# A 2-layer transformer with an RWKV block: the end of a finished channel tile put behind the next tile's first inversion matrices, bias rows copied in one piece, bias loads issued behind evacuations

## The reference, cut to what matters

```python
for l in range(2):                                   # first kind
    mod = silu(c) @ ada_w[l] + ada_b[l]              # 6 x 1024 numbers: shift, scale, gate, twice
    h = rms_norm(x) * (1 + sc_m) + sh_m
    proj = h @ w_in[l]                               # q, k, v of three attentions, three gates
    o_na  = neighborhood_attention(...)              # 4 heads; bias rpb (4,15,31) by row and column offset
    o_mla, o_gqa = latent and grouped attention
    x = x + g_m * ((sig(ga)*(o_na@wa) + sig(gb)*(o_mla@wb) + sig(gc)*(o_gqa@wc)) @ w_out)
    x = x + g_f * ffn(rms_norm(x) * (1 + sc_f) + sh_f)
x = rms_norm(x)
p = rms_norm_2(x) @ w_in_2                           # second kind
y_a = b_a * conv3(c_a * x_a);  y_b = rg_lru(conv4(x_b)) * gelu(g_b)
# RWKV-7: state = state*w_t + (state@-kk)(kk*a) + v k ; y = state@r, chunks of 128 tokens
yc = group_norm(y)*lnx_g + lnx_b + bonus;  y_c = yc * g_c
x = x + (gate_a*y_a + gate_b*y_b + gate_c*y_c) @ w_out_2
x = x + relu(rms_norm_2(x) @ w1)**2 @ w2;  out = rms_norm_2(x)
```

## Time and profile before

| | |
|---|---|
| median of 3 runs | 3166.22 us (3163.53 to 3168.85) |
| profiled execution | 3169.7 us; its span, first to last instruction, 3167.9 us |
| PE busy | 2930.3 us, 92% |
| DVE busy | 1698.2 us, 54% |
| ACT busy | 698.0 us, 22% |
| POOL busy | 1279.5 us, 40% |
| mean granted TensorE clock | 0.973 |

### The profile page before, as it was taken

One profiled execution on the slowest core, in us unless ns is written; L12 is line 12 of the kernel. 1 busy time (PEld: TensorE's weight loads), 2 busy tenths in 40 slices (PEclk: granted clock), 3 DMA queues, 4 the chain that ended last, 5 costly groups with the idle time before them and its releaser, 6 DMA issues.

```text
span 3167.9 us, 44134 instructions
## 1 busy us (share of the span) xinstructions
PE 2930.3 (92%) x18104; PEld 2265.4 (72%) x18104; DVE 1698.2 (54%) x2263; ACT 698.0 (22%) x1183; POOL 1279.5 (40%) x940
## 2 busy tenths in 40 slices
PE   2899988999998999999999969999999999999997
PEld 1666666787786767777888757777777777778786
DVE  4488775566513776445443274665465466463352
ACT  2343220200002443201000033223233323220000
POOL 1323334455564333354555522333233323345553
PEclk8899999999999999999999989999999999999999
DMA  8644556577766233364555532333233333445553
GB/s 271 180 136 141 190 200 200 178 239 236 235 218 176 93 93 122 120 199 162 193 192 197 198 109 99 106 119 121 89 125 114 112 104 117 142 159 190 182 192 113
DMA packets 174631, 503.85 MB, mean 159 GB/s; under 512 B 41206, under 2 KB 56566, under 8 KB 174198
## 3 DMA queue, kind: packets, MB, share of 16 engines
q1 hardware_dynamic: 82800, 274.75, 26.7%
q0 software_dynamic: 67392, 218.40, 19.5%
q10 hardware_dynamic: 24262, 8.21, 1.6%
HBM read 280.76 MB, written 6.06 MB: 91 GB/s over the span
## 4 chain that ended last, share of the span: by engine, by line
PE 78%; DVE 10%; DMA 4%; issue 3%; POOL 2%; ACT 2%; ACTq 1%; SPq 0%; DVEq 0%; POOLq 0%
PE ps L327 22%; PE ps L328 20%; PE ps L329 20%; DMA raw<-in_weights_dram 4%; PE ps L1184 3%; PE ps L1015 2%; POOL wR L531 2%; PE ps L1025 2%; PE ps L1035 2%; PE ps L1229 1%; DVE work L1465 1%; DVE dB L1889 1%; DVE kB L1901 1%; PE ps L1328 1%; DVE yB L1862 1%
## 5 line engine op out<-in xcount | busy, mean ns | idle before, releaser
L327 PE MATMUL ps<-hR,wR 128*128 128x512 f32 x2320 | 960.6, 414 | 117.2 <-DVE hR L1472 52.1
L531 POOL TENSOR_TENSOR wR<-raw,wR 128x1024 fp32r<-128x1024 f32 (+3 forms) x468 | 1016.2, 2171 | 69.9 <-DMA wR<-raw 52.4
L522 POOL DMA_DIRECT2D wR<-raw x468 | 267.4, 571 | 1783.8 <-issue 1321.8
L328 PE MATMUL ps<-hR,wR 128*128 128x512 f32 x2320 | 916.7, 395 | 0.0
L329 PE MATMUL ps<-hR,wR 128*128 128x512 f32 x2320 | 916.1, 395 | 0.0
L327 PEld LDWEIGHTS ps<-hR,wR 128*128 128x128 f32 x2320 | 443.5, 191 | 249.5 <-issue 134.0
L329 PEld LDWEIGHTS ps<-hR,wR 128*128 128x128 f32 x2320 | 442.6, 191 | 97.2
L328 PEld LDWEIGHTS ps<-hR,wR 128*128 128x128 f32 x2320 | 444.6, 192 | 86.6 <-issue 4.8
L1428 DVE CUSTOM_DVE_ANT_0 raw<-raw,cs 128x1024 f32<-128x1024 f32 x96 | 165.0, 1728 | 72.1 <-DMA raw<-in_weights_dram 65.7
L557 ACT ACTIVATE sq<-xT 128x512 f32<-128x512 f32 x56 | 35.4, 633 | 493.8 <-DVE xT L1479 341.9
L1479 DVE SCALAR_TENSOR_TENSOR xT<-ps,lm,xT 128x512 f32<-128x512 f32 x32 | 24.0, 751 | 223.1 <-PE ps L329 223.1
(11 more groups left out here) (358 smaller groups left out, 4153.7 us busy)
## 6 DMA issues: line engine op xcount, KB each, us to landing
raw<-in_weights_dram SPq DMA_DIRECT2D x490, 512.0 KB, 3.3
wR<-raw POOLq DMA_DIRECT2D x394, 512.0 KB, 2.9
raw<-in_weights_dram SPq DMA_DIRECT2D x50, 128.0 KB, 2.9
wR<-raw POOLq DMA_DIRECT2D x50, 128.0 KB, 2.0
raw<-in_weights_dram SPq DMA_DIRECT2D x16, 256.0 KB, 3.2
wR<-raw POOLq DMA_DIRECT2D x16, 256.0 KB, 2.6
bias_toeplitz<-bias_rows ACTq DMA_DIRECT2D x8, 476.2 KB, 15.8
bias<-bias_toeplitz ACTq DMA_DIRECT2D x16, 224.0 KB, 5.7
```

The costliest lines, as they stand in the source:

```text
L327: mm(out, w_hi, r_hi, start=first, stop=False)
L328: mm(out, w_hi, r_lo, start=False, stop=False)
L522: pool.dma_start(wR[:, u, 0, 0:cols], raw[:, r % RING, 0:cols]).then_inc(hi_ready[u], 16)
L531: nc.gpsimd.tensor_tensor(wR[:, u, 1, 0:cols], raw[:, r % RING, 0:cols], wR[:, u, 0, 0:cols], ALU.subtract).then_inc(tile_ready, 1)
```

## The change

1. **Order of the stream.** Weight tile 0 stands before mod tile 14, weight tile 1 behind mod tile 15. The two rope tables (512 KB each) are no longer among the nine inputs that SP issues behind the first four tiles but are issued just before weight tile 3, with a semaphore of their own for which DVE waits before it uses the bias.
2. **Bias rows.** The four `toeplitz` DMAs of a layer become one: 64 copies of the layer's 60 rows, each a piece of 7620 numbers. The sliding by one number a partition is now in the reading pattern of the loads into `bias` (same shape, 64x14x64).
3. **Bias loads** are issued by ACT behind the evacuation of product 1 (four) and of product 2 (four), in both layers; layer 1's copy behind the evacuation of product 4.
4. **First two products of layer 0**: product 1 follows product 0 four steps behind. Layer 1 keeps the old order.
5. **RWKV**: `finish` is cut in two. `finish_y` (norm, bonus, times g) stays; the four instructions after it (gate, sum, two for `mR`) go behind the identity add. ACT takes g after `g_used`, and waits for `m_done` before it takes ca. The product for the bonus (`bnB`) goes from before the first X mask to behind the first T add. PE takes 22 steps before the LT matrices and 6 behind the L matrices, not 21 and 7.

```diff
-RAW.insert(N_FIRST - 1, ("tile", 1))
-RAW.insert(N_FIRST - 3, ("tile", 0))
+RAW.insert(N_FIRST - 2, ("tile", 0))
 for g_ in range(G_USED):
-    if g_ > 1:
+    if g_:
         RAW.append(("tile", g_))
...
+                if r == RAW_AT["tile", 3]:
+                    for dst, src in ((tab, tables1["axial"]), (tabm, tables1["rope"])):
+                        sp.dma_start(dst[:], src).then_inc(s_tab, 16)
...
-            def toeplitz(l):
-                for lh in range(4 * l, 4 * l + 4):
-                    act.dma_start(bass.AP(dram_toeplitz, GRID * 15 * SKEW * lh, [[SKEW, 15], [15 * SKEW + 1, GRID], [1, 127]]),
-                                  bass.AP(dram_bias, 127 * 15 * lh, [[127, 15], [0, GRID], [1, 127]])).then_inc(s_rows, 16)
+            def copy_rows(l):
+                act.dma_start(bass.AP(dram_copies, GRID * BIAS_ROWS * l, [[BIAS_ROWS, GRID], [1, BIAS_ROWS]]),
+                              bass.AP(dram_bias, BIAS_ROWS * l, [[0, GRID], [1, BIAS_ROWS]])).then_inc(s_rows, 16)
+            def load_bias(l, heads):
+                act.wait_ge(s_rows, 32 + 16 * (l + 1))
+                for h in heads:
+                    for half in range(2):
+                        first = GRID * BIAS_ROWS * l + (h * 15 + 1 - half) * 127 + GRID - 1
+                        act.dma_start(bias[64 * half:64 * half + 64, h],
+                                      bass.AP(dram_copies, first, [[BIAS_ROWS - 1, GRID], [127, 14], [1, GRID]])).then_inc(s_bias, 16)
...
                     if p in (2, 3):
                         turn(p - 2)
+                    if p in (1, 2):
+                        load_bias(l, (2 * p - 2, 2 * p - 1))
+                    if p == 4 and l == 0:
+                        copy_rows(1)
...
-                act.wait_ge(m_done, m + 1)
+                act.wait_ge(g_used, m) if m else None
                 take("g", m, gB[:])
...
+                act.wait_ge(m_done, m + 1)
                 take("ca", m, msum[:])
...
-            def pair_of_products(ts, p, H):
+            def pair_of_products(ts, p, H, lead=0):
+                slots, banks = {}, {}
+                for k in range(KD + lead):
+                    for j, kj in enumerate((k, k - lead)):
+                        if not 0 <= kj < KD:
+                            continue
+                        if kj == 0:
+                            slots[j], banks[j] = need_tile(Count(ts[j])), claim(Count(p + j))
+                        if j == 0:
+                            pe.wait_ge(h_ready, H + k + 1)
...
-                pair_of_products((TI, TI + 1), PR, H)
+                pair_of_products((TI, TI + 1), PR, H, 0 if l else 4)
...
-                fill(21)
+                fill(22)
                 pe.wait_ge(prep_ready, m + 1)
                 lt_blocks().then_inc(mat_ready, 1)
                 pe.wait_ge(y_sb, m) if m else None
                 l_blocks().then_inc(mat_ready, 1)
-                fill(7)
+                fill(6)
...
                 shift_in("k", m, 0, kB[:], W_MUK)
                 if m:
-                    finish(m - 1)
-                else:
-                    floor_k(0)
+                    finish_y(m - 1)
+                floor_k(m)
                 shift_in("v", m, 1, vB[:], W_MUV)
...
                 v.sync()
+                if m:
+                    finish(m - 1)
                 dve.wait_ge(shifted, 5 * m + 3)
-                STT(bnB[:], rB[:], vec(vec2, W_RK), kB[:], ALU.mult, ALU.mult).then_inc(bn_in, 1)
```

More of the change, by code:

```diff
@@ L19 @@
 GRID = 64
-SKEW = 127 + GRID - 1
+BIAS_ROWS = 4 * 15 * 127
 FFN = 2816
@@ L593, in _ @@
                 round_h(2 * KD * l, SH_M)
-                act.wait_ge(s_rows, 32 + 64 * (l + 1))
-                for half in range(2):
-                    for h in range(4):
-                        src = dram_toeplitz.ap()[l * 4 + h, :, 1 - half:15 - half, GRID - 1:127]
-                        act.dma_start(bias[64 * half:64 * half + 64, h], src).then_inc(s_bias, 16)
-                if l == 0:
-                    toeplitz(1)
                 def ended(p):
@@ L873, in h_lo @@
                 return hR[:, 1, k, :]
-            def pair_of_products(ts, p, H):
-                slots, banks = [need_tile(Count(t)) for t in ts], [claim(Count(p + j)) for j in range(2)]
-                for k in range(KD):
-                    pe.wait_ge(h_ready, H + k + 1)
-                    for j in range(2):
-                        mm = three_passes(MM, ps[:, banks[j], :], weight(slots[j], 0, k * P), weight(slots[j], 1, k * P),
-                                          h_hi(k), h_lo(k), k == 0, k == KD - 1)
-                        if k == KD - 1:
+            def pair_of_products(ts, p, H, lead=0):
[8 more added lines that the diff above has]
+                            pe.wait_ge(h_ready, H + k + 1)
+                        mm = three_passes(MM, ps[:, banks[j], :], weight(slots[j], 0, kj * P), weight(slots[j], 1, kj * P),
+                                          h_hi(kj), h_lo(kj), kj == 0, kj == KD - 1)
+                        if kj == KD - 1:
                             mm.then_inc(tile_used, 1)
@@ L2041, in _ @@
                 v.sync()
+            finish_y(KD - 1)
             finish(KD - 1)
```

29 lines of the change are left out of this document (15 added, 14 removed).

## The result

| | before | after |
|---|---|---|
| median | 3165.71 us (3163.53 to 3168.85, 4 runs) | 3117.61 us (3111.86 to 3124.59, 4 runs) |
| ratio | | 0.9845 (0.9821 to 0.9869) |
| profiled execution, span | 3169.7, 3167.9 us | 3111.9, 3110.0 us |

A forecast was written before the change was run, and what follows sets the result against it. PE, busy 92% of the span, was taken as the bound, with gains only in its waits or slow running. Layer 0's 28.5, layer 1's 3.5 and RWKV's 23.5 made 55.5 us: 3111 us, 8-in-10 range 3099 to 3130.

The forecast's parts named there:

- RWKV, the best step: RWKV tiles: waits of 4.0 us go, 1.1 come anew, 20.3 us over seven, plus 3.2 of clock: 23.5 us.
- The rival of 3127 us: RWKV: full subtractions on moved instructions or identity add make the new wait 2.8 us; RWKV brings 5 to 10; chance 0.13.
- Norm: Start of layer 0: last mod tile lands at 39.7 us, so the norm starts at 41.6, 14.3 earlier.
- 4.6 us go: Loads before layer 0's norm: the bias-row copy costs 5.0 us instead of 9.6, bringing the last mod tile earlier.
- First product: Layer 0: PE's first product starts at about 46 us; products 0 and 1 end at 66 instead of 76.3.
- The twelve DMAs: Layer 0 behind product 1: PE's 16.8 us wait during ACT's DMA issues goes whole, plus 2.4 us of slow clock.
- If one issue took as long as those in the 13.61 us it still fits: Layer 0 bias loads: four issues take 3.8 us within a 5.4 us product; one of 3.4 us would still fit.
- A long wait at the first scores: Sign of being wrong, layer 0: bias late at the first scores; 1 us was charged, up to 4 in the range.
- In layer 1 I had 3.5 us: Layer 1: the 3.8 us wait for ACT's evacuation goes, 0.3 us stays: 3.5 us (3 to 3.8).
- The copy does not sit on a few DMA engines: Slower rival, bias-row copy: it runs on one or two DMA engines, giving about 3170 us; chance 0.03.
- The mod tiles come no earlier: Rival, start of layer 0: copy as costly, weights crowded out or h held by collisions; 3124 us, chance 0.09.
- The port: Rival, port shared by DVE and GpSimd: DVE keeps it when it starts first; 3106 us, chance 0.02.

The follow-up runs named there:

- finish_in_three: Changed kernel with r's shift behind the identity add, gate and sum before the first X mask, both `mR` instructions behind the first T add: 3112.7 us.
- copy_alone: Kernel before with only the one-piece bias-row copy and its reading pattern, loads at their old places: 3156.28 us, ratio 0.9960.
- old_stream: Changed kernel with the old load order restored: weight tiles 0 and 1 and the rope tables at their old places; 3125.68 us, ratio 0.9871.
- after_again: The changed kernel run again, unchanged, for the spread of its runs: 3109.76 to 3125.95 us, ratio 0.9836.
- mask_halves: Changed kernel with two bias DMAs behind each of products 1 to 4, mask added in halves, layer 1's copy behind product 5: 3105.13 us, ratio 0.9806.
- tile0_early: Changed kernel with weight tile 0 one place earlier and POOL's first subtraction ahead of the second cast: 3124.05 us, ratio 0.9856.

## Why the prediction came out right, and what was off

**RWKV, the best step.** Waits of 4.0 us a tile gone, new ones of 1.5 instead of 1.1. Idle time fell by 19.5 us, forecast 20.3. The clock gave back 6.9 instead of 3.2 us: the slow stretches of the earlier trace rows are gone from tiles 1, 3 and 5. In sum 26.3 us against 23.5. The new wait is made otherwise than forecast. The 0.95 us for the X mask is close to the forecast 1.1, with the small subtraction in it. The 0.56 us for the identity add was in no term: there a full subtraction lies on the shift of r in every tile. With that shift moved away, in `finish_in_three`, this wait is gone. The rival of 3127 us wanted a full subtraction on the moved instructions or the identity add; it fell a few instructions earlier, where it costs 0.6 us a tile and not 2.4. That it fell there was not worked out, so the choice against the rival held partly by luck. (The rival's own figure should be 4.0 - 2.8 = 1.2 us a tile, not 1.4.)

**Norm: a right sum of two wrong terms.** Norm at 43.5 us, forecast 41.6, so 12.4 us earlier instead of 14.3. The copy cost 4.7 us of the engines as taken (5.0). But "4.6 us go" does not turn into a last load 4.6 us earlier: with the old order of the stream the copy gave 0.5 us (`copy_alone`) or 1.7 us (`old_stream`). The order of the stream gave the rest, about 11 us, where I had counted 9.7 for being free of the subtraction and of the tables. The step assumed that the DMA engines are the limit up to there; with four slots, a load is asked for only when a slot is free, and the last one waited for the subtraction. That time saved on the engines is spent waiting for slots fits these runs; no run had another number of slots.

**First product at 48.9, not 46.** I had the subtraction of tile 0 at 42.6. It began at 45.96, because tile 0's copy, issued at 39.67, landed only then, 6 us on, beside weight loads. It did not matter for the end: h bounded the pair (two collisions of 2.83 and 3.17 us as forecast), and product 1 was taken out at 66.04, forecast 66.

**The twelve DMAs: the failed step.** "If one issue took as long as those in the 13.61 us it still fits" allowed for one long issue; there were four. Three issues of 3.1 us each in the mean stand in a row behind one of 3.0, 12.4 us in all, against products of 5.4; but the evacuation of product 3 is wanted only when product 4 is done, so PE stood for no more than 1.9 us, and in `after_again` not at all. The cost of 0.96 us came from eight issues made while the weight stream stood still; the rows for issues among busy engines were those of 3.4 us. The landing was right as a distance, 7.6 us from the last issue to the mask (8.8 before), but that issue ended at 84 instead of 76, so the mask ended at 95.8 instead of 85 to 90. In layer 0 of the profiled execution that costs 1.9 us at product 5, 1.5 us at the mask, and a slow stretch behind the wait (granted clock 0.50 from 86.40 to 89.80); in `after_again` it is all at the mask, 6.6 us. A long wait at the first scores was named among the signs of being wrong, and it came. The first maxima came 24.4 us earlier (22.9 in `after_again`), where 28.5 was forecast for this place; with `mask_halves` they come 30.1 earlier. In layer 1 I had 3.5 us and the mechanism was missed altogether: the wait goes, the mask takes its place, and nothing is left (50.7 against 50.3 us), until the loads are spread and the mask is halved.

**Where the forecast was lucky.** The profile has the RWKV part begin 31.6 us earlier, and 28.5 + 3.5 = 32.0 was forecast. But only 24.4 us of that were won up to the first maxima, and layer 1 up to its first maxima gave none. The missing 7.1 us lie between the first maxima and layer 1, 5.6 of them in the attention of layer 0 (470.7 to 465.1 us), a stage that took 471.5 us in `after_again` and 462 to 474 us over all thirteen profiles. No term of the forecast speaks of it, and no part of the change is in it. In `after_again` the RWKV part begins 17.7 us earlier. The terms as measured, 24.4 + 0 + 26.3 = 50.7 us, are near the gain by the medians (48.1 us, and 50.6 in `after_again`): the start fell short by 7.6 us, RWKV gave 2.8 more, and 3117.6 us is inside the range with that. (The low ends of the terms add up to 36 us, not 43, so the forecast's own range ends at 3130 and not at 3123.)

**The rivals.** No large new wait at the X mask (longest 1.3 us; the subtraction that could have made it is told above). The copy does not sit on a few DMA engines: it landed in 10.7 us. "The mod tiles come no earlier" is `copy_alone`, not this change. The port: an h instruction of DVE that began at 52.98 took 3.17 us, beside POOL's subtraction from 53.24. By the profile's starts it was first and did not keep its pace, as in the earlier trace rows; so it is with the shift of r (1961.58 against 1962.05). The Trainium skill, "SBUF — State Buffer", SBUF: two separate sides, has the first to start keep the port; this trace differs, and the measurement decides.

## What to carry to other kernels

The price of a DMA issue is read where the new place lies, not where the old one lay: among busy engines a queue that was given eight small-piece transfers, four by four, held its engine for some 3 us a piece once the first few were out, and the same ones two by two held it for 2.2 us a pair at most in one run and 3.6 in another, which a product hides. When transfers are moved out of the way of one wait, look up who reads what they bring; an earlier consumer and a later producer can cancel, as in layer 1. And with a ring of few slots, ask which release lets the last load start: the order of the ring was worth 10.7 us at the norm, 4.7 us of transfer time saved 0.5 to 1.7. Last, when a stage that the forecast says nothing of differs by 6 us between two executions of one program, a sum that meets one profile is no proof of its terms; compare stage by stage.

## What the hardware showed that was not expected

- Eight runs of the changed program fall in two groups of times, some 12 us apart, with the granted clock of the attention stage at 0.97 in one profile and 0.95 in the other, and the program before spreads as widely (3156.9 to 3171.6). A ratio from four runs is good to about 0.25%.
- A copy inside DRAM in pieces of 30 KB took half the engines' time of one in pieces of 508 bytes (q10: 15.7% of 30 us, 4.7 us, against 32.0%, 9.6 us), and the last of the loads beside it was used 0.5 to 1.7 us earlier.
- Pieces of 256 bytes fill the engines at 169 GB/s (1.35 MB in 8 us at a share of 109.8%), where weights ran at 387 alone; so a bias load takes some twice the engines' time of as many bytes of weights.
- A rounded copy of 512 KB from SBUF to SBUF lands in 6 us beside weight loads and took 8 us in `tile0_early`, against 4.2 us in the median of the first 60 us before.
- POOL's subtraction of 2.4 us stretches a DVE instruction of 0.75 us to 3.1 to 3.5 us even where DVE's started 0.15 to 0.5 us before it: the shift of r, in all seven tiles.
